# Three gate tile pairs of a decoder trunk as seven quadrant products each, with the branch pairs behind them

## The reference

```python
h = rms_norm(x, g_mix[l])
proj = jnp.einsum('bld,de->ble', h, w_in[l])
rq, rk, rv, rg, mq, mk, mv, gate_r, gate_a = split_proj(proj)
...
ro = (head_rms(ro).reshape(B, L, R_V) * jax.nn.silu(rg.astype(jnp.float32))).astype(x.dtype)
...
merged = (jax.nn.sigmoid(gate_r) * (ro @ w_br_ret[l])
          + jax.nn.sigmoid(gate_a) * (mo @ w_br_att[l]))
x = x + merged @ w_out[l]
```

## Time and profile before

| | us |
|---|---|
| median of 3 runs | 1979.16 |
| lowest and highest | 1978.31, 1979.25 |
| the profiled execution, by itself | 1980.56 |
| its span in the trace | 1978.9 |
| PE busy | 1959.4 |
| DVE busy | 1217.7 |
| ACT busy | 849.1 |

### The profile page before, as it was taken

How to read it: one execution, slowest core, us unless ns; L and a number is a source line. 1 busy time by engine, 2 the same in 40 slices (tenths; PEclk the granted TensorE clock), 3 DMA queues, 4 the chain that set the end, 5 groups by cost and what they waited for, 6 DMA issues and landing times.

```text
span 1978.9 us, 41246 instructions
## 1 busy us (share of the span) xinstructions
PE 1959.4 (99%) x16851; PEld 1838.7 (93%) x16851; DVE 1217.7 (62%) x1952; ACT 849.1 (43%) x1365; POOL 133.6 (7%) x221
## 2 busy tenths in 40 slices
PE   8999999999999999999999999999999999999999
PEld 8968978999999999999998798799899999999999
DVE  6475413347445888988674743143664458889876
ACT  4365522332224354555434754233332344555544
POOL 0001120011000000000000012200110000000000
PEclk9999999999999999999999999999999999999999
DMA  6327683245334343333344277812443342433332
GB/s 211 125 69 220 203 286 99 86 150 168 121 108 131 86 130 91 103 106 89 106 156 131 86 217 234 284 56 91 166 146 112 98 137 79 132 107 104 89 113 83
DMA packets 254563, 262.55 MB, mean 133 GB/s; under 512 B 13706, under 2 KB 218674, under 8 KB 253874
## 3 DMA queue, kind: packets, MB, share of 16 engines
q1 hardware_dynamic: 235186, 190.69, 31.2%
q0 software_dynamic: 19072, 69.22, 10.7%
q10 hardware_dynamic: 128, 0.15, 0.0%
HBM read 234.98 MB, written 25.03 MB: 131 GB/s over the span
## 4 chain that ended last, share of the span: by engine, by line
PE 93%; DVE 4%; ACT 1%; issue 1%; DMA 1%; POOLq 0%; POOL 0%; DVEq 0%; ACTq 0%
PE PS L804 38%; PE PS L1221 21%; PE PS L784 3%; PE PS L939 3%; PE PS L785 3%; PE PS L786 3%; PE PS L764 2%; PE PS L765 2%; PE PS L766 2%; PE PS L979 2%; PE PS L1025 1%; PE PS L709 1%; PE PS L917 1%; PE PS L887 1%; PE PS L901 1%
## 5 line engine op out<-in xcount | busy, mean ns | idle before, releaser
L1803 DVE TENSOR_TENSOR WL<-RAW,WH 128x2048 fp32r<-128x2048 f32 (+2 forms) x88 | 188.7, 2144 | 116.8 <-ACT WH L1315 116.7
L804 PE MATMUL PS<-XH,WH 128*128 128x272 f32 x1152 | 243.1, 292 | 0.6
L804 PE MATMUL PS<-XL,WH 128*128 128x272 f32 x1152 | 238.0, 288 | 0.0
L804 PE MATMUL PS<-XH,WL 128*128 128x272 f32 x1152 | 237.9, 288 | 0.0
L804 PEld LDWEIGHTS PS<-XH,WH 128*128 128x128 f32 x1152 | 180.6, 188 | 7.8 <-issue 5.2
L804 PEld LDWEIGHTS PS<-XL,WH 128*128 128x128 f32 x1152 | 181.0, 189 | 0.0
L1315 ACT ACTIVATE WH<-RAW 128x2048 fp32r<-128x2048 f32 (+2 forms) x96 | 172.6, 1798 | 19.2 <-PE PS L804 18.6
L804 PEld LDWEIGHTS PS<-XH,WL 128*128 128x128 f32 x1152 | 180.4, 189 | 0.0
L1221 PE MATMUL PS<-KQ,CH 128*128 128x272 f32 x1088 | 158.3, 288 | 1.4 <-DVE KQ L2251 1.4
L784 PE MATMUL PS<-WH,XH 128*128 128x256 f32 x512 | 152.1, 297 | 0.0
L1221 PEld LDWEIGHTS PS<-KQ,CH 128*128 128x128 f32 x1088 | 145.0, 188 | 2.2 <-issue 2.2
(11 more groups left out here) (427 smaller groups left out, 4926.4 us busy)
## 6 DMA issues: line engine op xcount, KB each, us to landing
RAW<-in_w_in SPq DMA_DIRECT2D x106, 512.0 KB, 4.7
RAW<-in_w_gu SPq DMA_DIRECT2D x128, 256.0 KB, 3.9
PG<-in_cache_k SPq DMA_DIRECT2D x64, 256.0 KB, 3.3
PG<-in_cache_k POOLq DMA_DIRECT2D x64, 256.0 KB, 3.4
RAW<-in_w_down SPq DMA_DIRECT2D x64, 256.0 KB, 3.9
RAW<-in_w_gu SPq DMA_DIRECT2D x24, 512.0 KB, 5.1
PG<-in_cache_v SPq DMA_DIRECT2D x44, 256.0 KB, 3.5
PG<-in_cache_v POOLq DMA_DIRECT2D x44, 256.0 KB, 4.2
```

The costliest lines, as they stand in the source:

```text
L804: last = pe.matmul(PS[:, 2 * pair + h, 0:HALF], w[:, i, c0:c0 + P], block[:, h * HALF:(h + 1) * HALF], start=first and i == 0 and a == 0, ...
L1803: dve.tensor_tensor(WL[:, slot, 0:n], RAW[:, slot, 0:n], WH[:, slot, 0:n].bitcast(F32), ALU.subtract).then_inc(lo_ready, 1)
```

## The change

Gate pair 0 and branch pair 0 stay as they are. Gate pairs 1 to 3 become three steps of seven products (`gr_seven(g)`, g = 0 to 2), one right behind the other; branch pairs 1 to 3 follow. The gates of pairs 1 to 3 are kept as sigmoids in a new buffer `SG` until their branch tiles come.

- Products 1, 4 and 7 use the quadrants of `XH`, `XL` as they are. Products 2, 3, 5 and 6 use four sums of x quadrants: POOL loads x from `XTD` into `XR` in four pieces of 544 KB, after `ss_done` and, piece by piece, after the state transfers that free the region; ACT multiplies it by the gain in eight copies; DVE makes the four sums in place, ACT their high halves (`SH`), DVE their low halves (`SL`, in place).
- The weights of a step come as four quadrants in four transfers of 256 KB. For each step ACT and DVE split three quadrants as they are (128x1536), DVE makes four sums of 128x512, and two pairs of sums (128x1024 each) are split.
- Each product has 4 blocks x 3 matmuls of 128x128 on 272 columns. Product 1 waits for the low half of the three quadrants (`gr_la`), product 2 for that of the first two sums (`gr_l12`), product 5 for that of the last two (`split_ready`). Products 3, 5 and 7 wait for a copy by ACT of an earlier partial result.
- The first branch unit after them is split in two halves, since its slot is in use until the last step ends.

In the diff below, helpers whose name says what they do are left out: `gr_a_high` and `gr_a_low` are the split of three quadrants, `gr_t12_*` and `gr_t34_*` those of the sums, `gr_copy` the copies, `x_sum` and `x_low` a sum of x quadrants and its low half, `gr_second` and `gr_first` the reading of a step's two result tiles, `gr_sig` the sigmoid into `SG`, `merged`, `merged_high` and `merged_low` what the loop `branch_ret` did with a branch tile.

```diff
+    XR, SL = at("XR", [P, KT, N], F32, GREG + 8 * N), at("SL", [P, KT, N], F32R, GREG + 8 * N)
+    SH = [at(f"SH{n}", [P, HK, HALF], F32R, o) for n, o in
+          enumerate((GREG + 40 * N, GREG + 40 * N + QUADS, R0, R0 + QUADS), 1)]
+    T12G = at("T12G", [P, 2, 512], F32R, ROREG + 4 * KT * N)
...
-            with sp.Fori(0, 4) as i:
-                full(U0["br_ret"] + 2 * i, 0, w_in, KT, C_GR + i * UC)
-                full(U0["br_ret"] + 2 * i + 1, 1, w_br_ret, KT, i * UC)
+            full(U0["br_ret"], 0, w_in, KT, C_GR)
+            full(U0["br_ret"] + 1, 1, w_br_ret, KT, 0)
+            for g in range(NGR):
+                dst, at_c = raw_chunks(g % 2), w_chunks(g % 2)
+                def gr_quad(name):
+                    r, c = int(name[0]) - 1, int(name[1]) - 1
+                    col = C_GR + (g + 1) * UC + c * P
+                    return (dst[:, at_c[name], :].rearrange("p (k c) -> p k c", c=P),
+                            rows(w_in, r * HK, HK)[:, :, col:col + P])
+                unit(U0["br_ret"] + 2 + g, g % 2, [gr_quad("11"), gr_quad("22")])
+                for name in ("21", "12"):
+                    d, c = gr_quad(name)
+                    sp.dma_start(d, c).then_inc(landed_gr[g % 2], 16)
+            for i in range(1, 4):
+                full(U0["br_ret"] + 4 + i, i % 2, w_br_ret, KT, i * UC)
...
+            pool.wait_ge(ss_done, lay * 8 + 8)
+            for i in range(4):
+                if i:
+                    pool.wait_ge(sn_out[i - 1], lay * 32 + 32)
+                pool.dma_start(XR[:, 2 * i:2 * i + 2, :], XTD.ap()[:, 2 * i:2 * i + 2, :]).then_inc(xr_in[i], 16)
...
-            with pe.Fori(1, 4) as i:
-                unit2(U0["br_ret"] + 2 * i, 0, T0["br_ret"] + 4 * i, kk, x)
-                unit2(U0["br_ret"] + 2 * i + 1, 1, T0["br_ret"] + 4 * i + 2, kk, (ROH, ROL))
...
+                pair12, pair34 = [gr_t12(g, low) for low in range(2)], [gr_t34(low) for low in range(2)]
+                pe.wait_ge(gr_la, lay * NGR + g + 1)
+                pe.wait_ge(tile_free, lay * NT + tile)
+                product(1, a_chunk("11"), a_bank, start=True).then_inc(gr_prod, 1)
+                pe.wait_ge(gr_l12, lay * NGR + g + 1)
+                product(2, t_chunk(pair12, t1), f_bank, start=True).then_inc(gr_prod, 1)
+                pe.wait_ge(gr_copied, lay * (4 * NGR) + 4 * g + 1)
+                product(3, t_chunk(pair12, t2), a_bank).then_inc(gr_prod, 1)
+                product(4, a_chunk("21"), c_bank).then_inc(gr_prod, 1)
+                split_ready(U0["br_ret"] + 2 + g)
+                pe.wait_ge(gr_copied, lay * (4 * NGR) + 4 * g + 3)
+                product(5, t_chunk(pair34, 0), a_bank).then_inc(gr_prod, 1)
+                product(6, a_chunk("22"), f_bank).then_inc(gr_prod, 1)
+                pe.wait_ge(gr_copied, lay * (4 * NGR) + 4 * g + 4)
+                product(7, t_chunk(pair34, 1), a_bank).then_inc(tile_done, 2)
+            for g in range(NGR):
+                gr_seven(g)
+            pe.wait_ge(half_lo, lay + 1)
+            for m in range(2):
+                feature_tile(T0["br_ret"] + 10 + m, 2 + m, 1, UC, m * P, kk, (ROH, ROL), final=False, part=kk[:4])
+            split_ready(U0["br_ret"] + 5)
+            for m in range(2):
+                feature_tile(T0["br_ret"] + 10 + m, 2 + m, 1, UC, m * P, kk, (ROH, ROL), first=False, part=kk[4:])
+            for i in range(2):
+                unit2(U0["br_ret"] + 6 + i, i, T0["br_ret"] + 12 + 2 * i, kk, (ROH, ROL))
...
+            sig(T0["br_ret"], 0, 0, 0)
+            for i in range(4):
+                act.wait_ge(xr_in[i], lay * 16 + 16)
+                for k in (2 * i, 2 * i + 1):
+                    scale = act.activation(XR[:, k, :], XR[:, k, :], ACT.Copy, scale=GT[:, 8 * lay + k:8 * lay + k + 1])
+            scale.then_inc(xr_scaled, 1)
+            gr_a_high(0)
+            act.wait_ge(sn_out[2], lay * 32 + 32)
+            act.wait_ge(sn_out[3], lay * 32 + 32)
+            for n, (r, c) in enumerate(((1, 1), (0, 0), (0, 1), (1, 0)), 1):
+                act.wait_ge(xs_sum, lay * 4 + (1, 3, 2, 4)[n - 1])
+                act.activation(SH[n - 1][:], x_quad(XR, r, c), ACT.Copy).then_inc(xs_hi, 1)
+                if n == 2:
+                    gr_t12_high(0)
+            sig(T0["br_ret"] + 1, 1, 1, 0)
+            act.wait_ge(x_lo, lay * NX + X0["rg"] + KT)
+            for g in range(NGR):
+                b = 4 * (g % 2)
+                gr_t34_high(g)
+                gr_copy(g, PS[:, b, 0:HALF], b + 1, 1)
+                if g == 1:
+                    gr_a_high(2)
+                gr_copy(g, PS[:, b + 3, 0:HALF], b + 2, 2)
+                if g == 0:
+                    act.wait_ge(tile_free, lay * NT + T0["br_ret"] + 6)
+                else:
+                    act.wait_ge(gr_up, lay * (2 * NGR) + 2 * g - 1)
+                gr_copy(g, EB[:, 1, 0:HALF], b + 1, 3)
+                if g == 0:
+                    gr_a_high(1)
+                for k in (2 * g, 2 * g + 1):
+                    if g == 0:
+                        merged_high(k)
+                    else:
+                        gr_sig(k)
+                gr_copy(g, EB[:, 1, HALF:N], b + 1, 5)
+                if g < NGR - 1:
+                    gr_t12_high(g + 1)
+            act.wait_ge(landed[1], (lay * NU // 2 + (U0["br_ret"] + 5) // 2 + 1) * 32)
+            half_high(0)
+            gr_step_done(NGR - 1)
+            half_high(1)
+            gr_sig(6)
+            gr_sig(7)
+            for i in range(1, 4):
+                split(U0["br_ret"] + 5 + i, (i + 1) % 2, 8 * UC, (tile_done, lay * NT + T0["br_ret"] + 8 + 2 * i))
+                merged_high(2 * i)
+                merged_high(2 * i + 1)
...
+            def gr_sums(g):
+                r, c = raw_chunks(g % 2), w_chunks(g % 2)
+                n = lay * (4 * NGR) + 4 * g
+                b11, b12, b21, b22 = (r[:, c[q], :] for q in ("11", "12", "21", "22"))
+                dve.wait_ge(gr_la, lay * NGR + g + 1)
+                dve.tensor_tensor(b11, b11, b12, ALU.subtract).then_inc(gr_sum, 1)
+                dve.wait_ge(gr_sum, n + 1)
+                dve.tensor_tensor(b12, b22, b12, ALU.subtract).then_inc(gr_sum, 1)
+                dve.wait_ge(gr_sum, n + 2)
+                dve.tensor_tensor(b22, b22, b11, ALU.add).then_inc(gr_sum, 1)
+                dve.wait_ge(gr_sum, n + 3)
+                dve.tensor_tensor(b21, b21, b22, ALU.subtract).then_inc(gr_sum, 1)
...
+            for m in range(2):
+                scaled(T0["br_ret"] + m, m, EA[:, m, :])
+            dve.wait_ge(xr_scaled, lay + 1)
+            x_sum(1, (1, 1), (0, 1), (1, 1), ALU.add)
+            x_sum(2, (0, 1), (0, 0), (0, 1), ALU.subtract)
+            x_sum(3, (0, 0), (1, 1), (0, 0), ALU.subtract)
+            x_sum(4, (1, 0), (0, 0), (1, 0), ALU.subtract)
+            gr_a_low(0)
+            gr_sums(0)
+            x_low(1, 1, 1)
+            x_low(2, 0, 0)
+            gr_t12_low(0)
+            x_low(3, 0, 1)
+            x_low(4, 1, 0)
+            for m in range(2):
+                merged(0, m, T0["br_ret"] + 2 + m, 2 + m, EB[:, m, :])
+            gr_t34_low(0)
+            merged_low(0)
+            merged_low(1)
+            gr_a_low(1)
+            gr_sums(1)
+            gr_t12_low(1)
+            for g in range(NGR - 1):
+                gr_second(g)
+                gr_t34_low(g + 1)
+                gr_first(g)
+                if g + 2 < NGR:
+                    gr_a_low(g + 2)
+                    gr_sums(g + 2)
+                    gr_t12_low(g + 2)
+            half_low(0)
+            gr_second(NGR - 1)
+            half_low(1)
+            gr_first(NGR - 1)
+            for i in range(1, 4):
+                split(U0["br_ret"] + 5 + i, (i + 1) % 2, 8 * UC)
+                for m in range(2):
+                    merged(i, m, T0["br_ret"] + 8 + 2 * i + m, 2 * (i % 2) + m, SG[:, 2 * i + m, :])
+                    merged_low(2 * i + m)
```

More of the change, by code:

```diff
@@ L81 @@
 NPAIR = NQ // 2
+NGR = 3
 HK = KT // 2
@@ L1165, in _, with gr_seven, a_chunk, t_chunk @@
             unit2(U0["br_ret"] + 1, 1, T0["br_ret"] + 2, kk, (ROH, ROL))
-            with pe.Fori(1, 4) as i:
-                unit2(U0["br_ret"] + 2 * i, 0, T0["br_ret"] + 4 * i, kk, x)
-                unit2(U0["br_ret"] + 2 * i + 1, 1, T0["br_ret"] + 4 * i + 2, kk, (ROH, ROL))
+            def gr_seven(g):
+                tile, j = T0["br_ret"] + 4 + 2 * g, g % 2
+                at_c = w_chunks(j)
+                c_bank, a_bank, f_bank = 4 * j, 4 * j + 1, 4 * j + 2
+                t1, t2 = (0, 1) if j else (1, 0)
+                def a_chunk(name):
+                    return [gr_a(g, low)[:, at_c[name] - 1, :] for low in range(2)]
+                def t_chunk(pair, n):
+                    return [t[:, n, :] for t in pair]
+                def moving(n, k, low):
+                    if n in (1, 4, 7):
+                        r, c = {1: (0, 0), 4: (1, 0), 7: (1, 1)}[n]
```

(37 more changed lines are left out.)

78 lines of the change are left out of this document (75 added, 3 removed).

## The result

The changed kernel took **1991.9 us** (median of 4 runs, 1991.0 to 1992.1) beside 1979.2 us before (median of 4): a ratio of 1.0064, 95% interval 1.0047 to 1.0082, so 12.7 us slower. The profiled execution took 1991.0 us (span 1989.3) against 1980.6 (span 1978.9).

The account below looks back on a forecast made before the run. PE, busy 99% of the span, was taken as the bound. Per layer, 10.05 us of waits less 4.5 saved, plus clock falls of 0.3 and 0.85, made 6.7, 13.4 in all: 1992.5 us, range 1986.5 to 2001.

Parts of the forecast that it names:

- a second fall of the clock: Behind step 1's 2.1 us wait: between 0 and 1.7 us lost a layer, taken as 0.85.
- product 1 late: Step 0: PE waits from 506.33 to 507.45 for the low half of the three direct weight quadrants, 1.1 us.
- product 2 late: Step 0: PE waits until 513.9 for the first weight sums and x sums, 4.95 us.
- product 5 late, clock at 1.00: Step 0: PE waits until 520.3 for the low half of the last two weight sums, 1.9 us.
- step 1 late, clock at 1.00: Product 2 of step 1 waits for the low half of its first two weight sums, ready at 528.4: 2.1 us.
- what the fall behind the long wait adds: Step 0, products 2 to 4 at a lowered clock: mostly hidden, some 0.3 us come through ACT's copy 3.
- saving of three products: One product of 12 matmuls, 1.50 us, saved in each of three gate pairs: 4.5 us a layer, 9.0 in all.
- DVE's line: Step 0: x scaled by 500.5, then sums and low halves in one DVE line, low halves ending 507.45, 513.9, 520.3.
- Much slower by a late fetch: Rival: x's four pieces arrive one behind the other, x ready at 507.8, 7.3 us a layer, 2007; 12 in 100 with clock.
- Much slower by the clock: Rival: two falls of 1.7 us a layer unhidden beyond the forecast's 1.15, 1999.5; 12 in 100 together with late fetch.
- A small loss through a shorter DVE line: Rival: more overlap on DVE; 1983.6 with a third of the waits gone, 1980.2 with half; 8 in 100.
- Faster through DVE's slack: Rival: sums ready in time, all waits of a layer under 4.5 us, only saved matmuls remain, 1970; 5 in 100.

Follow-up runs that it names:

- e6: Changed kernel with gate pair 1 and branch pair 1 in the old form, only pairs 2 and 3 as seven-product steps behind them: 1975.6 us, ratio 0.9984.
- e4: Changed kernel with 36 unused matmuls filling PE's long wait ahead of product 2 of step 0: 1992.1 us, ratio 1.0070.
- e9: Changed kernel with unused matmuls in both long waits, 36 ahead of product 2 of step 0 and 16 in step 1: 1991.3 us, ratio 1.0066.
- e1: Changed kernel without the fetch of x from DRAM; the scaled copies read XH instead: 1992.6 us, ratio 1.0075.
- e3: Changed kernel with the four x sums and the eight scaled copies cut to 16 elements: 1979.7 us, ratio 1.0005.
- e7: Changed kernel reordered: step 0's weight lows and sums before the x sums, step 1's weights before the merged low halves: 1982.4 us, ratio 1.0020.
- e5: Changed kernel with only step 0's weight splits and sums moved ahead of the scaling and sums of x: 1987.1 us, ratio 1.0039.
- e2: Changed kernel with only the four x sums on DVE cut to 16 elements: 1986.3 us, ratio 1.0046.

## Why the prediction was right, and where it was off

Forecast 1992.5, measured 1991.9; forecast 6.7 us a layer, found 5.8 and 6.0. The difference is about the 0.85 us that were set aside for a second fall of the clock. What an idle in brackets costs PE, and what three pairs save, can be measured cleanly in e6, where one wait stands alone. PE's timeline, layer 0: the first matmul of the steps, the last before the wait, the one that waited and its successor, and the first branch matmul behind the steps:

```profile
530.43 0.29 PE L1241 MATMUL PS<-XH,CH 128*128 128x272 f32 x1
...
542.36 0.29 PE L1241 MATMUL PS<-XH,CH 128*128 128x272 f32 x1
543.35 0.40 PE L1241 MATMUL PS<-SH,T12G 128*128 128x272 f32 x1 [0.70 <-DVE CH L2360]
543.58 0.29 PE L1241 MATMUL PS<-SL,T12G 128*128 128x272 f32 x1
...
552.49 0.42 PE L849 MATMUL PS<-ROH,WH 128*128 128x272 f32 x2
```

From start to start the wait takes 543.35 - 542.36 = 0.99 us where 0.125 is usual, and the next start comes 0.1 us late too: 0.96 us lost for a bracket of 0.70, so **a wait costs its bracket and 0.26 us**. The two steps take 552.49 - 530.43 = 22.06 us; less 0.96 that is 10.55 each for 84 matmuls, against 96 x 0.1248 = 11.98 of a pair in the old form: **1.43 us saved a pair**, 4.3 a layer. With these, term by term:

| term, us a layer | predicted | measured |
|---|---|---|
| product 1 late | 1.1 | 0.98 + 0.26 = 1.24 |
| product 2 late | 4.95 | 4.66 + 0.26 = 4.92 |
| product 5 late, clock at 1.00 | 1.9 | 1.54 + 0.26 = 1.80 (e4) |
| step 1 late, clock at 1.00 | 2.1 | 1.76 + 0.26 = 2.02 (e4, layer 0) |
| what the fall behind the long wait adds | 0.3 | 148.2 - 148.0 = 0.2 (after against e4, layer 0; 0.4 in layer 1 against e9) |
| a second fall, in step 1 | 0.85 | 0 in both layers of after |
| saving of three products | -4.5 | -4.3 |
| sum | 6.7 | 5.9 |

The layers took 5.8 and 6.0 us more.

**DVE's line** was the step that mattered, and it held. The scaling's end was put at 500.5, less 1.87 is 498.6, and DVE's first sum starts at 498.61. The three low halves were to end at 507.45, 513.9 and 520.3, less 1.87 is 505.6, 512.0 and 518.4; PE starts the products that need them at 505.60, 512.04 and 518.37. Step 1's 528.4 becomes 526.5, and the product starts at 526.69. Durations of the same shapes from elsewhere in the trace, added up in the order of the code, were enough.

**The saving** was mis-sized by 0.2 us a layer: a step runs at 10.55 / 84 = 0.1256 us a matmul, not 0.1248. The products follow each other through copies of partial results, and that may be where the difference lies; it was not tested.

**The clock.** The mechanism was forecast right: the fall behind the long wait stretches products 2 to 4, and product 5's idle shrinks from 1.54 us to 0.23 in return. The 0.85 us for a second fall was a mean of two outcomes that each occur, none of which is 0.85. In after's profile neither layer paid it; e4's layer 1 shows it. All four executions of the changed kernel read the same mean granted clock, 0.997; whether one of them had a second fall is not known.

**Luck in the median.** The forecast for a profiled execution, 1994.0, is 3.0 us above the 1991.0 measured, while that for the median is off by 0.6. The profiled execution of before was 1.4 us above its median, that of after 0.9 us below. Their spans differ by 10.4 us: 11.8 in the two layers and 0.5 between them, less the 1.87 us by which the first layer's stage starts earlier. The layers are the fairer test of the mechanism, and there the forecast was 0.7 to 0.9 us a layer too high.

**The rivals.** Much slower by a late fetch: e1 excludes it. Much slower by the clock: after against e9 the falls are worth 0.2 and 0.4 us of a layer. The rival's 1999.5 also puts 3.4 us of falls on top of the 1.15 that already stand for them; without that it is 1997.2. The Trainium skill, "TensorE: Matmul & The Clock Gate", section "HAM oscillation — how this bites in real kernels", describes a matmul loop with a wait of some 3 to 5 us in each pass, behind which PE starts again at the slow clock each time. The traces agree for the wait of that length: behind 4.66 and 4.67 us the clock fell in 4 of 4 cases. After's waits of 0.98 and 2.04 us left it at 1.00. A small loss through a shorter DVE line: the four waits came to 9.98 us a layer at a clock of 1.00 (the first four rows of the table) against 10.05 forecast. Faster through DVE's slack: its point was all waits of a layer under the saving. The runs bear that out, with 0.26 us for each wait and the clock counted in. e3 has 0.39 + 1.88 + 0.5 + 1.6 = 4.4 against 4.3 and is a draw; e7's layer 0 has 2.72 + 1.56 + 0.5 = 4.8 and is 0.5 us slower than before; e6 has 0.96 against 2.9 and is faster. What the rival left out was that the room may be had by a later place as well as by an earlier x.

## What to carry to other kernels

A form that saves matmuls but needs its operands prepared pays from the moment at which the preparation fits beside PE work already there; the first use of it should stand late enough for that, even at the price of using it less often (two pairs late beat three pairs at once by 16 us here). Write down the one line of the preparing engine, operation by operation, with what it waits for, and lay it beside the clock times at which PE wants each part: here that gave each late start to 0.2 us. And inside such a line put first what depends on nothing late (the weights), and last what depends on the late input.

## What the runs showed of the clock

Not expected was how irregular the fall of the granted clock is behind idles of about 2 us. Every PE idle of over 0.3 us in the changed stage that another engine ended, over both layers of the ten profiled runs of the changed kernel and its variants, and whether the granted clock was down behind it before the next such idle:

| idle, us | cases | clock fell |
|---|---|---|
| 0.34 to 1.56 | 21 | 0 |
| 1.74 to 2.73 | 18 | 10 |
| 4.66, 4.67 | 4 | 4 |

Two stretches of one run, e7, behind idles of 2.72 us in layer 0 and 2.73 in layer 1 (the same instruction, the same kernel):

```profile
509.61:514.61 5.00, 4.77 (x36) 4.55 (x36) 4.93 (x6) 1.93 (x5) 0.00 (x0) 1.00 0.00 0
1483.34:1488.34 5.00, 5.00 (x27) 5.00 (x28) 4.93 (x6) 1.53 (x4) 0.00 (x0) 0.66 0.00 0
```

The length of the idle doesn't decide it in this band: 1.74 us fell once and 2.72 us did not. Behind idles of the middle band the fall itself is the same each time, 0.66 over 5 us as in the earlier trace rows, and 27 matmuls done in them where 39 or 40 are otherwise, some 1.6 us. For an estimate, a wait of this length has to carry 0 or 1.6 us, not a value between. Behind the long idle it varies, since the clock can fall while PE still waits: 0.70 over 5 us in after's layer 0, and 0.57 in e1's layer 1, where it was down 2.4 us before the restart and the layer took 148.8 us.

The fall is not confined to the changed stage. In e5's profiled run PE waited 1.59 us for a transfer, between the two layers' stages, and the clock fell:

```profile
1288.10 1.07 PE L1068 MATMUL PS<-PG,PTS 128*32 128x512 f32 x8 [1.59 <-DMA PG<-in_cache_v]
...
1290.00:1296.00 6.00, 6.00 (x40) 5.37 (x40) 2.18 (x5) 1.37 (x4) 0.00 (x0) 0.50 0.00 0
```

The same instruction waited 1.58 us in e2 and the clock stayed at 1.00. This run took 1991.1 us, 4.0 above e5's median; from the end of the first layer to the start of the second it took 833.8 us where the other nine profiled runs of the changed kernel and its variants took 830.0 to 831.1. The spread of the times points the same way: e2 ranges over 5.7 us and e5 over 6.3 us between their 4 runs, e9, with both waits filled, over 0.9 us in 5. The mean granted clock is on record for every execution: e2's slowest run reads 0.994 where its others read 0.996 and 0.997, e5's slowest 0.995 where its others read 0.997, and all five of e9 read 0.999. Where in an execution the clock was down, only the profiled ones show.
